# Head mixers: high weight part first, first turn in the transposition banks, first loads laid by quarters

## The reference

```python
def moba_mixer(xn, w_qkv, w_o, cos, sin):        # stage A, the first of the program
    qkv = (xn @ w_qkv).reshape(B, S, 3, N_HEADS, HEAD_DIM)
    q = apply_rope(qkv[:, :, 0], cos, sin)
    k = apply_rope(qkv[:, :, 1], cos, sin)
    o = moba_attention(q, k, qkv[:, :, 2])        # 256 positions: one block, so causal attention
    return o.reshape(B, S, N_HEADS * HEAD_DIM) @ w_o

def chunk_attention(h, w_qkv, q_norm, k_norm, rel_table, w_o):   # stage DD, the seventh of eight
    q, k, v = jnp.split(h @ w_qkv, 3, axis=-1)
    q = head_rmsnorm(q.reshape(B, S, N_HEADS_2, HEAD_DIM_2), q_norm)
    k = head_rmsnorm(k.reshape(B, S, N_HEADS_2, HEAD_DIM_2), k_norm)
    ...                                           # softmax over a band of chunks, with a bias
    return o @ w_o
```

## Time and profile before

| | us |
|---|---|
| median of three runs | 1083.37 |
| lowest, highest | 1083.12, 1083.43 |
| the profiled execution | 1083.64 |
| its span in the trace | 1081.8 |
| outside of the span | 1.84 |
| PE busy | 1074.4 |
| DVE busy | 833.3 |
| ACT busy | 654.8 |

### The profile page before, as it was taken

How to read it: one execution, slowest core, us unless ns; L and a number is a source line. 1 busy time by engine, 2 the same in 40 slices (tenths; PEclk the granted TensorE clock), 3 DMA queues, 4 the chain that set the end, 5 groups by cost and what they waited for, 6 DMA issues and landing times.

```text
span 1081.8 us, 16475 instructions
## 1 busy us (share of the span) xinstructions
PE 1074.4 (99%) x6642; PEld 943.2 (87%) x6642; DVE 833.3 (77%) x1352; ACT 654.8 (61%) x919; POOL 1.3 (0%) x8
## 2 busy tenths in 40 slices
PE   9999999999999999999999999999999999999998
PEld 7778988888898898888889888888977798888888
DVE  6876699877577679988667999776658859998852
ACT  6656567655467765766456677654546855776540
POOL 0000000000000000000000000000000000000000
PEclk9999999999999999999999999999999999999999
DMA  8553346556436046655653366555565434665540
GB/s 303 190 194 118 126 166 228 210 183 215 147 133 223 3 156 224 232 197 185 211 188 118 122 229 224 193 209 191 168 193 180 141 118 153 230 208 195 204 151 30
DMA packets 31948, 191.68 MB, mean 177 GB/s; under 512 B 4480, under 2 KB 5888, under 8 KB 12032
## 3 DMA queue, kind: packets, MB, share of 16 engines
q1 hardware_dynamic: 31872, 190.63, 51.1%
HBM read 189.56 MB, written 1.05 MB: 176 GB/s over the span
## 4 chain that ended last, share of the span: by engine, by line
PE 96%; ACT 1%; DMA 1%; DVE 1%; SPq 0%; issue 0%; DVEq 0%; ACTq 0%
PE banks L421 20%; PE TB L421 12%; PE banks L423 11%; PE SB L421 10%; PE banks L389 8%; PE banks L391 8%; PE banks L390 8%; PE TB L423 6%; PE SB L423 6%; PE banks L582 2%; PE TB L557 2%; PE SB L544 1%; DMA raw<-in_a_kq 1%; PE SB L935 1%; PE banks L677 1%; PE SB L940 0%
## 5 line engine op out<-in xcount | busy, mean ns | idle before, releaser
L1553 DVE TENSOR_TENSOR wlo<-raw,whi 128x2048 fp32r<-128x2048 f32 (+2 forms) x180 | 395.3, 2201 | 77.5 <-ACT whi L1069 77.5
L1069 ACT ACTIVATE whi<-raw 128x2048 fp32r<-128x2048 f32 (+2 forms) x180 | 330.2, 1839 | 88.4 <-PE banks L423 28.5
L421 PE MATMUL banks<-xx,whi 128*128 128x512 f32 x704 | 247.3, 391 | 0.0
L423 PE MATMUL banks<-xx,wlo 128*128 128x256 f32 x704 | 198.5, 282 | 0.0
L421 PEld LDWEIGHTS banks<-xx,whi 128*128 128x128 f32 x704 | 132.2, 188 | 27.7
L421 PE MATMUL TB<-xx,whi 128*128 128x512 f32 x384 | 135.5, 390 | 0.0
L423 PEld LDWEIGHTS banks<-xx,wlo 128*128 128x128 f32 x704 | 133.1, 189 | 0.1
L421 PE MATMUL SB<-xx,whi 128*128 128x512 f32 x320 | 111.8, 390 | 0.0
L423 PE MATMUL TB<-xx,wlo 128*128 128x256 f32 x384 | 108.3, 282 | 0.0
L389 PE MATMUL banks<-whi,xx 128*128 128x512 f32 (+3 forms) x240 | 93.2, 388 | 2.2 <-ACT kT L1250 1.5
L421 PE MATMUL banks<-hx,whi 128*128 128x512 f32 x264 | 91.9, 390 | 0.0
(11 more groups left out here) (210 smaller groups left out, 1918.3 us busy)
## 6 DMA issues: line engine op xcount, KB each, us to landing
raw<-in_gate SPq DMA_DIRECT2D x44, 1024.0 KB, 4.8
raw<-in_up SPq DMA_DIRECT2D x44, 1024.0 KB, 4.8
raw<-in_down SPq DMA_DIRECT2D x32, 1024.0 KB, 4.8
raw<-in_down SPq DMA_DIRECT2D x16, 768.0 KB, 4.4
raw<-in_d_kq SPq DMA_DIRECT2D x8, 1024.0 KB, 4.8
raw<-in_a_kq SPq DMA_DIRECT2D x6, 1024.0 KB, 5.9
raw<-in_a_o SPq DMA_DIRECT2D x4, 1024.0 KB, 4.7
raw<-in_b_o SPq DMA_DIRECT2D x4, 1024.0 KB, 4.7
```

The lines of the kernel that those rows point to most:

```text
L421: e.matmul(po[:, 0:512], wh[:, k, sl], a[:, kk, :, :].rearrange("p w s -> p (w s)"), start=start, stop=stop, skip_group_check=True)
L423: return e.matmul(po[:, 0:256], wl[:, k, sl], a[:, kk, 0, :], start=False, stop=stop, skip_group_check=True)
L1069: e.activation(whi[n % RING][:, 0:nk * w], raw[n % RAW][:, 0:nk * w], ACT.Copy).then_inc(s_hi, 1)
L1553: e.tensor_tensor(wlo[n % RING][:, 0:nk * w], raw[n % RAW][:, 0:nk * w], whi[n % RING][:, 0:nk * w].bitcast(F32), ALU.subtract).then_inc(s ...
```

## The change

1. **Order within rows.** `row_of` is replaced by `high` (high by high, low by high, both with `whi`) and `low` (high by low, with `wlo`). `both_halves` issues for each k four matmuls of `high` and then two of `low`; `quarter` eight of `high` and then four of `low`. The wait for `wlo` stands before `low`; ahead of `high` there is a wait for `whi` alone.
2. **First turn.** `turn_over(0)` writes to `TB` (`turn_bank`), and ACT copies from there. Slot 2 waits for the readers of slot 0 only (`s_nat` in A, `s_cp` in DD). PE's order becomes, in A, `quarter(2, 0, 0)`, `quarter(2, 0, 1)`, `turn_over(0)`, `quarter(2, 1, 0)`, `pair_scores(0)`, `quarter(2, 1, 1)`; in DD `quarter(2, 0, 0)`, `turn_over(0)`, `quarter(2, 0, 1)`, `pair_scores(0)`. On ACT `hi(u + 6)` (in A) moves behind the two `value` copies and `hi(u + 7)` (in DD) ahead of `turned_over(0)`. On DVE, in A, `lo(u + 4)` and `lo(u + 5)` go ahead of `rotated(0, 1)`.
3. **Sums of squares.** In A `norm_sums` stands one k later, behind k = 0 of slot 1. ACT squares the first two blocks already after k = 1.
4. **Loads.** The three first units lie in memory by quarters (256 KB in one piece, where rows of 2 KB were 8 KB apart). The first x load is cut in two (`x0` of 132 KB with the gains, `x1` of 128 KB behind the first weight quarter), so SP issues one load more; the others are contiguous.
5. **Warm-up** has 9 matmuls where it had 12.

```diff
-                    for i in range(12):
+                    for i in range(9):
...
+                def high(i, h, k):
...
+                    e.matmul(po, xx[:, k, 0, sl], wh[:, k % 4, :], start=k == 0, stop=False, skip_group_check=True)
+                    e.matmul(po, xx[:, k, 1, sl], wh[:, k % 4, :], start=False, stop=False, skip_group_check=True)
+                def low(i, h, k):
...
+                    return e.matmul(slot_bank(s, i, h)[:, :], xx[:, k, 0, sl], wl[:, k % 4, :], start=False,
+                                    stop=k == KD - 1, skip_group_check=True)
...
+                        if i == 1 and k == (1 if s == A else 0):
+                            norm_sums(s)
...
+                        if by_quarters:
+                            high_quarter_here(n, k % 4)
                         elif k % 4 == 0:
-                            weights_here(u + 2 * i + k // 4)
-                        first_half = row_of(i, 0, k)
-                        last = row_of(i, 1, k)
+                            high_here(n)
+                        high(i, 0, k)
+                        high(i, 1, k)
+                        if by_quarters:
+                            quarter_here(n, k % 4)
+                        elif k % 4 == 0:
+                            weights_here(n)
+                        first_half = low(i, 0, k)
+                        last = low(i, 1, k)
...
+                        if i == 2:
+                            e.wait_ge(s_nat if s == A else s_cp, n_kh(0, h))
...
+        def turn_bank(s, g, q):
+            return TB[:, q, :] if g == 0 else slot_bank(s, KQ_SLOT[g], q)
...
             for k in range(KD):
-                e.wait_ge(s_x[k // 2], 16)
+                e.wait_ge(s_x[k if k < 2 else k // 2 + 1], 16)
                 split_x(A, k)
                 hi_quarter(k // 4, k % 4)
+                if k == 1:
+                    squares(A, 0)
             for q in range(4):
-                squares(A, q)
+                if q:
+                    squares(A, q)
                 hi_quarter(2, q)
...
-    a["x"] = np.concatenate([chan(i["norm_mix"][0]), i["x"][0].T.reshape(KD, 128, S).transpose(1, 0, 2).reshape(128, KD * S)], 1)
+    x = i["x"][0].T.reshape(KD, 128, S)
+    a["x0"] = np.concatenate([chan(i["norm_mix"][0]), x[0]], 1)
+    a["x1"] = x[1]
+    a["x"] = x[2:].reshape(3, 2, 128, S).transpose(0, 2, 1, 3).reshape(3, 128, 512)
...
+    first = np.stack([a["a_kq"][0], a["a_kq"][1], a["a_v"][0]])
+    a["a_first"] = first.reshape(RAW, 128, 4, 512).transpose(0, 2, 1, 3)
```

More of the change, by code:

```diff
@@ L112, in build @@
         s_first = [[sem(f"s_first{n}_{q}") for q in range(4)] for n in range(RAW)]
-        s_x = [sem(f"s_x{q}") for q in range(4)]
+        s_x = [sem(f"s_x{q}") for q in range(5)]
         s_con, s_vec, s_win, s_bias, s_out = (
@@ L394, in weights_here, with high_here, high_quarter_here @@
                 e.wait_ge(s_lo, n + 1)
+            def high_here(n):
+                e.wait_ge(s_hi, n + 1)
+            def high_quarter_here(n, q):
+                if q < 3:
+                    e.wait_ge(s_hq, 3 * n + q + 1)
+                else:
+                    high_here(n)
             def quarter_here(n, q):
@@ L628, in both_halves @@
+                def low(i, h, k):
+                    _, wl = unit(u + 2 * i + k // 4)
+                    sl = slice(h * 128, (h + 1) * 128)
+                    return e.matmul(slot_bank(s, i, h)[:, :], xx[:, k, 0, sl], wl[:, k % 4, :], start=False,
+                                    stop=k == KD - 1, skip_group_check=True)
                 def both_halves(i):
                     for k in range(KD):
+                        n = u + 2 * i + k // 4
+                        by_quarters = s == A and n < RAW
+                        if i == 1 and k == (1 if s == A else 0):
+                            norm_sums(s)
@@ L644, in quarter @@
                 def quarter(i, h, part):
+                    n = u + 2 * i + part
                     if h == 0:
[L647 removed]
+                        high_here(n)
                     if part == 0:
[L649 removed]
+                        if i == 2:
+                            e.wait_ge(s_nat if s == A else s_cp, n_kh(0, h))
+                        elif i == 3:
                             e.wait_ge(s_vv, n_vv(s, 0, h))
                         else:
[L652 removed]
+                            e.wait_ge(s_te, n_te(s, i - 3, 1 - h))
                         if i >= 4 and h == 1:
@@ L655, in quarter @@
                     for k in range(4 * part, 4 * part + 4):
-                        last = row_of(i, h, k)
+                        high(i, h, k)
+                    if h == 0:
+                        weights_here(n)
+                    for k in range(4 * part, 4 * part + 4):
+                        last = low(i, h, k)
                     if h == 1:
@@ L693, in heads_mixer @@
                 both_halves(0)
-                norm_sums(s)
                 both_halves(1)
-                turn_over(0)
+                quarter(2, 0, 0)
                 if s == A:
-                    quarter(2, 0, 0)
                     quarter(2, 0, 1)
+                    turn_over(0)
+                    quarter(2, 1, 0)
                     pair_scores(0)
-                    quarter(2, 1, 0)
                     quarter(2, 1, 1)
@@ L1250, in turned_over @@
                         e.activation(dst[:, :, :].rearrange("p c s -> p (c s)"),
-                                     slot_bank(s, KQ_SLOT[g], 1 - part)[:, :], ACT.Copy, **kw).then_inc(s_te, 1)
+                                     turn_bank(s, g, 1 - part)[:, :], ACT.Copy, **kw).then_inc(s_te, 1)
                 if s == A:
                     hi(u + 5)
-                    hi(u + 6)
                     value(0, 0)
                     value(0, 1)
+                    hi(u + 6)
                     turned_over(0)
@@ L1867, in heads_mixer @@
                     rotated(0, 0)
-                    rotated(0, 1)
                     lo(u + 4)
                     lo(u + 5)
+                    rotated(0, 1)
                     lo(u + 6)
```

26 lines of the change are left out of this document (13 added, 13 removed).

## The result

The changed kernel took 1079.8 us, median of 6 runs (1079.36 to 1080.1), beside 1083.91 for the kernel before, run in the same places (6 runs, 1083.12 to 1084.92). The ratio is 0.9961, 95% interval 0.9948 to 0.9974. The profiled execution has a span of 1078.2 us against 1081.8.

A forecast was written before the change was run, and what follows sets the result against it. PE's work was taken as the bound (busy 1074.4 of 1081.8 us), so only its standstills could be won. 0.97 + 0.74 + 1.11 + 0.74 = 3.56 us took the profiled 1083.64 to 1080.1, median 1079.8; range 1078.6 to 1081.5.

The forecast's parts named there:

- Term a: Start: rows begin on `whi` alone, k = 2 waits for the third quarter, landing 0.2 us earlier; gain 0.97 us.
- Term b: Sums of squares in A: squared earlier, asked one k later, so PE no longer waits; gain 0.74 us.
- six k: Matmuls said to cover DVE's work behind the sums before the change, given as 4 x 1.40 = 5.6 us.
- Terms c and d: First turns in A and DD: no wait for `kT`, each turn 0.87 us; gains 1.11 and 0.74 us.
- Rival 1: Start: third quarter so early that PE does not wait; 0.3 to 1 us more, 1079.5 to 1078.6; chance 0.15.
- Rival 3: Sums, or unit 3's low part, still stop PE; price up to 0.74 us, 1080.6; chance 0.08.
- Rival 4: PE idles after the shorter warm-up, clock rises late; at 10.3 us a further 1.0 to 1.3 lost, 1080.9; chance 0.07.
- Rival 5: New order in A meets a wait counted as covered; price about 1.2 us, 1081.0; chance 0.09.
- Rival 6: Rows in both mixers lose pace as the stationary operand alternates; with 15 ns, loss 8.6, 1088.4 us; chance 0.03.

The follow-up runs named there:

- b_again2: The kernel before, unchanged, measured and profiled once more: profiled span 1083.5 us, mean clock 0.998.
- e7: Changed kernel with ACT's first square moved ahead of the second weight quarter's conversion: 1079.5 us, ratio 0.996.
- e6: Changed kernel with 12 warm-up matmuls as before, instead of 9: 1079.89 us.
- e1: Changed kernel with the first three weight units in memory as before, rows 8 KB apart: 1080.56 us, ratio 0.9965.
- e10: Kernel before with only the first three weight units laid out by quarters, x loads whole: 1082.51 us, ratio 0.999.
- e4: Changed kernel with ACT's first square back behind the last x block: 1079.81 us, ratio 0.9961.
- e2: Changed kernel with rows again high, low, high, waiting for the low part first: 1080.68 us, ratio 0.9968.
- e3: Changed kernel with both first turns back in the slot's banks and the old orders on PE, ACT and DVE: 1084.91 us, ratio 1.0003.
- e5: Kernel before with only the change's first-turn part, banks and engine orders, in both mixers: 1081.66 us, ratio 0.998.
- e9: Changed kernel with 4 warm-up matmuls instead of 9: 1080.49 us.
- e8: e7 with PE's sums one k later still and DVE's `lo(u + 3)` ahead of `norm_col`: 1079.79 us, ratio 0.996.
- b_again: The kernel before, unchanged, measured and profiled once more: profiled span 1082.1 us, mean clock 1.000.

## Why the prediction came out

**The size.** Sum 3.56, measured 3.6 between the spans and 3.5 between 1079.8 and the 1083.27 of before at full clock. The median of before in this comparison is 0.54 higher than the one I started from, since three of its six runs lie above 1084.3. The prediction never named this part of the gain: in b_again2 a fall of the clock worth 1.5 us follows a long step at the sums, and the change removes that step.

**Term a, 0.97, measured 0.91, by another way.** I had the third quarter's load as what ends last. It was the second's: its conversion started at 6.97 instead of the forecast 5.94, so k = 1 started at 7.74, and k = 2 waited for ACT, which did a square and a split first. The load of 5.94 was one execution's value; over the profiled executions this conversion starts anywhere from 5.70 (e7) to 6.97, in before from 5.94 to 6.91. I treated a landing that scatters by one us as fixed. That term a came out near its forecast in an execution with an unusually late second quarter is in part luck. The first row came at 4.92, not 5.3: the half-sized x load let ACT start at 2.89 instead of 3.92. As said, nearly all of it was waited away (e6).

**The layout within term a.** I gave it 0.2 us with the remark that no row shows it. e1 and e10 show 0.8. That term a has its size is therefore no proof of its working: in e4 the second quarter is converted from 6.06 on and k = 2 starts at 8.32, and the sums still start at 19.16, then bound by the squares.

**Term b, 0.74, measured 0.91.** The last add ended at 18.98 (forecast 18.9), the sums started at 19.28 (19.2) with no wait. The step from the sums to the next row is 0.81 and not the 0.88 of before, and nothing was lost to the change of matmul type, where I had left 0.1. It is 0.81 wherever PE came to the sums without a wait, e2 with the old order of rows included, and 0.88 or 0.89 behind a wait (e1, e4, e10). What the later place costs I priced at unit 3's low part alone; that the copy behind the old turn hangs on the sums too, e3 showed. The "six k" of that paragraph is a slip: its own product, 4 x 1.40, has the four k that stood there before.

**Terms c and d, 1.11 and 0.74, measured 1.19 and 0.82.** The wait went as forecast, and its cover held: unit 5's low part ended at 31.98 (forecast 32.4), `rotated(0, 1)` at 33.97 (34.5), `hi(u + 6)` at 33.02 (33.6), before the turn at 35.57 (35.7). The 0.08 by which each exceeds its forecast is one wrong price: I took 0.87 from a turn that transposes follow. Followed by a row, it is 0.79, in A, in DD and in e5.

**The sum as a sum.** I added the terms as if each stood alone. e3 shows that a and b together are worth nothing without c and d, and the timelines say why: b moves PE ahead of a chain on ACT that hangs on the sums, and high first delays the value copies ahead of the turn in DD. A gain like a's, which brings the sums forward, is kept even with the old turn (e10). It did not matter for this change, which does all of them; it would have for a forecast of a part.

**The rivals.** Rival 1, no wait at k = 2, is what e4 did, and it gave nothing, because DVE's last add then ended last: its price of 0.3 to 1 us was wrong. Rival 3 did not happen, but the cover of unit 3's low part is what the order "high first" pays for: e2 loses it and waits. Rival 4 happened in e9, not here. Its price, 1.0 to 1.3 for a rise at 10.3 us, was 0.7 for one at 10.6, and its remark that the clock column does not show the start is right. Rival 5 did not happen. Rival 6 fell: 0.233 us a step in both orders. The range, 1078.6 to 1081.5, holds all experiments but e3, e5 and e10, which undo or leave out a part.

**Open.** The DMA rate of 121 GB/s between 5 and 6 us in the kernel after is no property of its x loads or its layout: e4, e6, e7, e8 and e9, with the same loads, have 293, 373, 262, 166 and 246 there, and before, b_again, b_again2 and e5, with the old ones, 268, 182, 236 and 193. Why single executions differ so much no run shows, nor how the layout makes its gain.

## What to carry to other kernels

Before adding up what several stalls are worth, ask of each wait further on what its releaser hangs on. If it hangs on the very event that you bring forward, the gain passes through (e10, sums 1.0 us earlier, 1.0 kept). If you only let PE run ahead of that event, the next wait takes it back (e3, sums one k later, 1.40 us waited at the turn). When the executions of one kernel lie in two groups, look at the mean clock of each, then for a stretch below 1.00 after a long standstill of PE: removing the standstill may then be worth more than its own length. Lay out contiguously what is loaded first, and take the landing of the first loads from several executions.

## What the runs showed of the hardware

- The granted clock fell to 0.50 for about 3.4 us after waits of PE of 1.36 us in b_again2 and 2.35 us in e3. It stayed at 1.00 after the longest ones of before (0.94), b_again (1.0), e5 (0.9), e1 and e7 (1.0 each). Each fall cost 1.5 us.
- At the start the steps of 0.43 us lasted until 10.4 us where PE had stood still for 1.6 us between warm-ups and first row (e9). Elsewhere their end scatters between executions: 6.7 after, 5.4 in e4, which has the same nine warm-ups; 7.2 before, and within the warm-ups in b_again2, which is the same kernel (24 matmuls in 4.89 us and not 5.49).
- Weight quarters of 256 KB laid as one block save about 0.8 us of the whole time against rows 8 KB apart (e1, e10).
- The start of the second quarter's conversion differs by 1.0 us between executions of the kernel before (5.94 to 6.91), and by 1.3 us between those of the kernels with the loads of the kernel after (5.70 to 6.97).
